# Layer 1's expert weights through one ring of 21 slots, and the gathers between the layers in another order

## What is computed

```python
def moe_ffn(h, router_w, router_b, w_gate, w_up, w_down):
    probs = jax.nn.softmax((h @ router_w).astype(jnp.float32), axis=-1)
    ...                      # the best group of 4 experts, and its top 2
    for e in range(N_EXPERTS):                                   # 16
        y_e = (jax.nn.silu(h @ w_gate[e]) * (h @ w_up[e])) @ w_down[e]
        out = out + combine[:, e:e + 1] * y_e
    return out
```

## Time and profile before

| | |
|---|---|
| median of three runs | 1805.14 us (1793.12 to 1809.05) |
| the profiled execution | 1814.62 us, its span 1813.0 us |
| busy: PE, DVE, ACT, POOL | 92%, 43%, 25%, 17% of the span |
| HBM read, written | 360.55 MB, 29.36 MB |
| layer 0's last block to layer 1's first product | about 1023 to 1066.71 us |
| layer 1's experts | about 1575 to 1799 us |

### The profile page before, as it was taken

One profiled execution on the slowest core, in us unless ns is written; L12 is line 12 of the kernel. 1 busy time (PEld: TensorE's weight loads), 2 busy tenths in 40 slices (PEclk: granted clock), 3 DMA queues, 4 the chain that ended last, 5 costly groups with the idle time before them and its releaser, 6 DMA issues.

```text
span 1813.0 us, 39477 instructions
## 1 busy us (share of the span) xinstructions
PE 1673.1 (92%) x15980; PEld 1064.6 (59%) x15980; DVE 788.7 (43%) x1901; ACT 461.9 (25%) x1015; POOL 303.9 (17%) x298
## 2 busy tenths in 40 slices
PE   5999998989999999999999888999889999899975
PEld 2467555554444444577777556667647888555543
DVE  3578863660110111543444377597664111423222
ACT  4011211552000000444444340111044000333321
POOL 0004341880000000210101210035355000000000
PEclk9999997999999999999999988998689999999998
DMA  9410369509211251489999843125571436599995
GB/s 390 123 67 23 134 243 315 99 18 339 107 69 70 101 224 70 194 328 383 390 383 391 328 172 99 47 84 202 204 140 48 156 146 255 236 392 395 410 410 223
DMA packets 105256, 381.19 MB, mean 210 GB/s; under 512 B 40592, under 2 KB 60304, under 8 KB 66000
## 3 DMA queue, kind: packets, MB, share of 16 engines
q1 hardware_dynamic: 85360, 335.44, 49.6%
q0 software_dynamic: 5648, 33.16, 5.3%
q10 hardware_dynamic: 14128, 10.85, 2.3%
HBM read 360.55 MB, written 29.36 MB: 215 GB/s over the span
## 4 chain that ended last, share of the span: by engine, by line
PE 75%; DVE 6%; DMA 6%; POOL 4%; SPq 3%; issue 3%; ACT 2%; ACTq 0%; DVEq 0%; POOLq 0%
PE tile_ps L661 61%; PE out_ps L661 6%; PE turn_ps L661 5%; SPq L573 3%; POOL arena L2189 3%; DMA h<-in_wpack 2%; DMA vn<-in_wpack 1%; PE turn_ps L986 1%; DMA ring<-in_wpack 1%; DVE arena L2008 1%; DMA x<-in_xT 1%; DVE smx L1990 1%; DVE arena L2100 1%; ACT arena L1459 1%; PE tile_ps L880 0%
## 5 line engine op out<-in xcount | busy, mean ns | idle before, releaser
L661 PE MATMUL tile_ps<-h,ring 128*128 128x512 f32 (+1 forms) x1312 | 478.0, 520 | 5.3 <-ACT h L1236 5.3
L661 PEld LDWEIGHTS tile_ps<-h,ring 128*128 128x128 f32 x1312 | 254.5, 195 | 212.4 <-issue 196.4
L661 PE MATMUL tile_ps<-arena,ring 128*128 128x512 f32 (+1 forms) x704 | 235.3, 486 | 2.4 <-issue 2.4
L661 PE MATMUL tile_ps<-arena 128*32 128x256 f32 (+2 forms) x3136 | 198.7, 341 | 9.1 <-DMA arena<-u_scratch 4.0
L661 PEld LDWEIGHTS tile_ps<-arena,ring 128*128 128x128 f32 x704 | 133.6, 190 | 95.3 <-issue 86.3
L661 PEld LDWEIGHTS tile_ps<-arena 128*32 128x32 f32 (+1 forms) x3136 | 132.0, 119 | 41.9 <-issue 10.3
L2189 POOL TENSOR_SCALAR arena<-arena,smx 128x512 f32<-128x512 f32 (+1 forms) x96 | 128.9, 1361 | 76.4 <-DVE smx L1996 76.1
L1431 ACT ACTIVATE arena<-tile_ps 128x512 f32<-128x512 f32 (+1 forms) x56 | 27.4, 490 | 347.3 <-PE tile_ps L661 347.3
L2030 DVE TENSOR_TENSOR arena<-tile_ps,arena 128x512 f32<-128x512 f32 (+1 forms) x32 | 17.9, 558 | 212.1 <-PE tile_ps L661 212.1
L661 PE MATMUL out_ps<-arena 64*128 64x64 f32 (+2 forms) x1032 | 95.6, 346 | 11.1 <-issue 10.9
L661 PEld LDWEIGHTS out_ps<-arena 64*128 64x128 f32 (+2 forms) x1032 | 77.9, 219 | 19.1 <-issue 19.0
(11 more groups left out here) (360 smaller groups left out, 2479.6 us busy)
## 6 DMA issues: line engine op xcount, KB each, us to landing
ring<-in_wpack SPq DMA_DIRECT2D x176, 1024.0 KB, 8.4
arena<-in_wpack SPq DMA_DIRECT2D x64, 1024.0 KB, 16.6
h<-in_wpack SPq DMA_DIRECT2D x15, 1024.0 KB, 20.1
qa<-in_wpack SPq DMA_DIRECT2D x12, 1024.0 KB, 16.9
qn<-in_wpack SPq DMA_DIRECT2D x12, 1024.0 KB, 18.9
kn<-in_wpack SPq DMA_DIRECT2D x12, 1024.0 KB, 20.8
vn<-in_wpack SPq DMA_DIRECT2D x12, 1024.0 KB, 23.6
x<-in_wpack SPq DMA_DIRECT2D x5, 1024.0 KB, 15.4
```

Of the source, the lines that this page charges most:

```text
L661: return nc.tensor.matmul(out, lhsT, rhs, start=start, stop=stop)
```

## The change

1. `FIFO`: layer 1's expert loads go through one ring of 21 slots in the order of use: load i lies in slot i mod 21. To the 18 slots come three: a dead piece of `arena` with the keys and values of grouped attention; the first 1024 columns of the constants with the working rows; the buffers of roots and squares with a quarter of `h`. Each is filled by two transfers of 512 KB. For this, small tiles are joined (`kv`, `work`, `roots`) and the constants are reordered so that those that are dead by then come first. Warm-up products read other columns of the constants.
2. Load i waits for the gate and up products, or the down products, of the expert that held slot i mod 21 before. Loads 18 and 19 wait for nothing but the router's tables, load 20 for `spread_full`.
3. Layer 1's ring slots 0 and 1 are loaded behind the late gathers too (`n == 0` where `n == 2` stood).
4. POOL issues three soon gathers, waits for `last_out`, then two late, the fourth soon, two late.
5. `load_root`: a root of one constant into a spare column, on ACT, behind the experts' loop of either layer.

```diff
+EXTRA = 3
+FIFO = SHELVES * RING + EXTRA
...
+        def fifo(i):
+
+            slots = (ring_slots + twin + rest_of[1] + extra_slots)[i % FIFO]
+            on, n, turn = i % FIFO // RING, i % FIFO % RING, i // FIFO
+            if on == SHELVES:
+                return slots, extra_in[n], 32 * (turn + 1)
...
-                    if l and n == 2:
+                    if l and n == 0:
                         for t in range(NTOK // P):
                             sp.wait_ge(rows_in[t], 16)
...
+                if l:
+                    freed = None
+                    for e in range(SHELVES, NEXP):
+                        weights = weights_of(sp, e)
+                        for n in range(RING):
+                            i = e * RING + n
+                            if i == FIFO - 1:
+                                sp.wait_ge(spread_full, 2)
+                            if i >= FIFO:
+                                held, part = divmod(i - FIFO, RING)
+                                if (held, part // 4) != freed:
+                                    freed = held, part // 4
+                                    sp.wait_ge((gu_full, down_full)[part // 4][l], before(sp, held + 1))
+                            slot, arrived, _ = fifo(i)
+                            if i % FIFO < SHELVES * RING:
+                                load(slot, arrived, weights + (first + n_static + n))
+                                continue
+                            for half in range(2):
+                                src = wpack[bass.ds(weights + (first + n_static + n), 1), :, half * D:(half + 1) * D]
+                                sp.dma_start(slot[half], src.rearrange("a p (k n) -> (a p) k n", k=4)).then_inc(arrived, 16)
+                    break
...
+            def load_root():
+
+                A(spare[:], c("eps"), ACT.Sqrt)
...
+                load_root()
                 for k in range(KD):
                     act.wait_ge(moe_done, l * NTOK // P * KD + k + 1)
...
+                load_root()
                 act.wait_ge(by_turn_done, 1)
...
+                for t in tiles[:3]:
+                    gather_soon(t)
+                pool.wait_ge(last_out, 16)
+                for t in tiles[:2]:
+                    gather_late(t)
+                gather_soon(tiles[3])
+                for t in tiles[2:]:
+                    gather_late(t)
```

More of the change, by code:

```diff
@@ L320, in backbone @@
         amuls = sb("amuls", [P, LAYERS, 2, KD, 2])
[L321 to L324 removed]
+        work = sb("work", [P, D])
+        csil, qrt, mrow = work[:, 0:256].rearrange("p (k n) -> p k n", k=KD), work[:, 256:512], work[:, 512:]
+        roots = sb("roots", [P, 2 * NTOK])
+        rstd, qsq = roots[:, 0:NTOK], roots[:, NTOK:]
         qrs = rstd
         raw = rstd
[L327 removed]
         qg8 = sb("qg8", [P, 1])
@@ L414, in backbone @@
         ht, a7 = cut(third + SLOT - NTOK // P * D, [NTOK // P, D])
-        assert early_slots <= a7 - NTOK // P * D and a8 <= a7 - NTOK // P * D and a7 - LAT // P * D <= third
+        spare_rows = a7 - NTOK // P * D - D
+        assert early_slots <= a7 - NTOK // P * D and a8 <= spare_rows and a7 - LAT // P * D <= third
         flat = lambda v: v[:].rearrange("p k n -> p (k n)")
@@ L435, in backbone @@
         diag = qsq[:].rearrange("p (t n) -> p t n", n=P)
+        in_quarters = lambda v: v.rearrange("p (k n) -> p k n", k=4)
+        extra_slots = [[in_quarters(arena[:, spare_rows:spare_rows + D]), in_quarters(kv[:])],
+                       [in_quarters(con[:, 0:D]), in_quarters(work[:])],
+                       [in_quarters(roots[:]), h[:, KD // 2:, CTX:]]]
         place_rows, part_rows, place_diag, part_diag = (h[:, k:k + 2, CTX:] for k in range(0, KD, 2))
@@ L556, in backbone @@
         ring_slots = [ring[:, n, :] for n in range(RING)]
+        def fifo(i):
[3 more added lines that the diff above has]
+                return slots, extra_in[n], 32 * (turn + 1)
+            if on == 0:
+                return slots, slot_in[n], 16 * (loads_before(1, n) + static_loads(1, n) + turn + 1)
+            in_layer_0 = sum(shelf(k)[0] == on for k in range(NEXP))
+            return slots, (twin_in, rest_in)[on - 1][n], 16 * (in_layer_0 + turn + 1)
         const_dram = const
@@ L757, in arrived @@
                 def arrived(e, n):
-                    pe.wait_ge(*shelf_in(l, e, n))
-                    slot = shelf_slots(l, e)[n]
-                    return slot if len(slot.shape) == 3 else slot.rearrange("p (k n) -> p k n", k=KD if n < 4 else 2)
+                    slot, here, loads = fifo(e * RING + n)
+                    pe.wait_ge(here, loads)
+                    if isinstance(slot, list):
+                        return lambda k: slot[k // 4][:, k % 4]
+                    v = slot if len(slot.shape) == 3 else slot.rearrange("p (k n) -> p k n", k=KD)
+                    return lambda k: v[:, k]
                 def pick_rows(r):
@@ L806, in down @@
                             for n in range(4):
-                                ins = mm(y[group(n)], hidT1[:, f, group(half)], slots[half][:, f, n * 256:(n + 1) * 256],
+                                ins = mm(y[group(n)], hidT1[:, f, group(half)], slots[half](4 * f + n),
                                          half + f == 0, half + f == 2)
@@ L2258, in _, with gather_soon @@
                 signal(4)
-                for t in tiles:
+                def gather_soon(t):
                     pool.indirect_dma_start(soon_rows[t], None, sorted_out,
@@ L2262, in _, with gather_late @@
                         .then_inc(soon_in[t], 16)
-                pool.wait_ge(last_out, 16)
-                for t in tiles:
+                def gather_late(t):
                     pool.indirect_dma_start(late_rows[t], None, sorted_out,
```

23 lines of the change are left out of this document (10 added, 13 removed).

## The result

The changed kernel took 1780.09 us in the median of 20 runs (1771.62 to 1807.99), the kernel before 1798.39 (1788.56 to 1810.58), 20 runs beside it. The ratio is **0.9885, 95% interval 0.9863 to 0.9908**: 1.15% faster, some 20.7 us of 1798 (the two medians lie 18.3 us apart). The forecast was 1790.0, within 1%; the time lies inside its range, and just on the other side of the 1% line.

The account below looks back on a forecast made before the run. In layer 1's experts PE ends up fed by the DMA stream alone, which bounds it. Ring 7.5 + seam 5.1 + table loads 2.6 = 15.2 us, 0.84% off the 1805.14 median, gives 1790.0 us; range 1777 to 1801.

Parts of the forecast that it names:

- The ring: Layer 1's experts: three extra slots let the weight stream start earlier, gaining 7.5 us.
- Two stalls stayed: PE's 5.88 us stall before expert 13 goes; those before experts 14 and 15 stay about as long.
- The halves: Extra slots' 24 loads of 512 KB in the experts' stream: charged nothing; rival of 7.9 us lost, chance 0.09.
- The seam: Between the layers: 5.1 us gained besides the table load; rival that layer 1 takes it back, chance 0.08.
- The store: POOL's last store at the seam lands in 2.9 us instead of 6.49; rival that it is no sooner, chance 0.18.
- The dummy root: At the seam, ACT's table load moves into its wait for the first gather, removing 1.28 us.
- DVE's second wait: At the seam, DVE's 0.83 us wait for PE's transposes shrinks by 0.3 us.
- The place in the order: At the seam, the first late gather issued one place sooner gains 1.27 us of the 4.8.
- ACT's store: Last block's store at the seam, awaited before the first late gather: 2.5 to 3.3 us beside gathers.
- The end: Behind the last block, the dummy root takes ACT's table load off the chain, gaining 1.28 us.
- PE's clock: Fuller clock at the seam's transposes counted within 0.3 us at DVE's second wait; no gain counted elsewhere.
- the far side: Whole kernel faster by over 1%, 18 us: chance 0.31, half of the forecast's own 0.62.

Follow-up runs that it names:

- c3: Kernel before with the new layout and three extra slots for layer 1's expert weights only, seam and table loads as before; ratio to before 0.9981.
- c5: The changed kernel, no edit, measured again beside the kernel before on another chip; ratio 0.9908.
- d1: The changed kernel, no edit, measured a third time beside the kernel before; ratio 0.9924.
- e1: The changed kernel, no edit, measured a fourth time beside the kernel before; ratio 0.9910.
- e2: The changed kernel plus four warm-up products at PE's 4.6 us gap in layer 1's mixer; ratio to the kernel before 0.9913.
- c1: Control: the kernel before, unchanged, against itself; ratio 1.0005.
- c2: Kernel before with only the joined tiles, reordered constants and warm-up products reading other columns, all loads as before; ratio to before 0.9992.
- c6: Kernel before with one edit, layer 1's first two loads held until behind the gathers; ratio to before 1.0008.
- c12: The changed kernel with the gathers in the old order, four soon ones first; ratio to the kernel before 0.9891.
- c8: Kernel before with only the two dummy roots (early table loads) added; ratio to before 0.9945.
- after: The changed kernel as first measured and profiled; 1780.09 us, ratio to the kernel before 0.9885.
- c10: The changed kernel without its three extra slots, so 18 instead of 21; ratio to the kernel before 0.9923.
- c4: Kernel before with the seam's part only: held layer 1 loads, new gather order and both dummy roots; ratio to before 0.9945.
- d3: The changed kernel without the dummy root at the seam, with 8 warm-up products instead of 5 before layer 1's first product; ratio to before 0.9908.
- d4: The changed kernel with nine more warm-up products at PE's waits in layer 1's mixer; ratio to the kernel before 0.9890.
- c7: Kernel before with only the new gather order (three soon, two late, one soon, two late); ratio to before 0.9982.
- d2: The changed kernel without the dummy root at the seam, the one at the end kept; ratio to the kernel before 0.9923.
- c9: Kernel before with only seven more warm-up products on PE, ahead of its waits for the gathers and layer 1's root; ratio to before 0.9978.

## Why the prediction came out as it did

**The ring: right, 7.5 forecast, about 7.** Expert 13's stretch is 23.8 us in the mean of eight traces with 18 slots turning, and 16.7 over the ten with 21 (all loads but the extra slots' whole). What returns is the stall of 5.88 us plus 1.1, which goes to PE's lower clock behind it (0.50 in 1752:1756; argued, not isolated). Two stalls stayed, as forecast, and the stream ran on at its old rate. Of the third, which the forecast had gone, 0.8 to 1.7 us were left in five of the ten traces (c3, c5, d1, e1, e2), each time for the first extra slot; where nothing was left the stretch is 16.0 and the gain 7.8. The halves, charged at nothing, cost about 1 us of it.

**The seam: right in its first cause, about 1 us less than forecast.** 5.1 + 1.28 = 6.4 were forecast; the four traces of the changed kernel have 25.6 us where c1, c2 and c3 have 30.9: 5.3. The store landed in 2.3 to 2.7 us (forecast 2.9), but that gave less than the forecast's 3.5: behind its issue the first late gather goes 2.5 us sooner than in c1 to c3 (8.2 and not 10.7 us), since the one trace read had the store at 6.49 and these at 5.1 to 5.3. The late gather itself brought 1.1 us that nobody had counted: DVE's first sum stands 5.3 us behind its issue and not 6.4. So 3.7 us in place of 4.8. By itself the hold is worth 4.0 with PE's clock (c6). The dummy root gives its 1.28, and DVE's second wait its 0.3 (3.13 us in the mean of the four, 3.41 before). The place in the order, counted at 1.27, gives nothing beside the other two (c12), because POOL then waits for ACT's store. The prediction's own times say as much: its three gathers are out at 1031.4 and the late one waits until 1033.0, so the fourth fits between. ACT's store took 3.5 to 4.0 us in the changed kernel, above the 2.5 to 3.3 that the prediction allowed for.

**The end: wrong.** "Both removed: 2.6 us" took the table load for 1.28 us at both places. At the end it gave 0.18 us (c8, and the trace of after). The rows of the chain put ACT's load behind ACT's squares; they did not show that PE's 16 products of these squares would be the next to hold the root. In the kernel before they stand at

```profile
1800.70 3.69 PE L661 MATMUL tile_ps<-h,con 128*128 128x256 f32 x16 [1.15 <-ACT h L1314]
```

and end at 1804.39, some 0.2 us before the load (1803.31 + 1.28). This is the term most plainly mis-sized: the prediction didn't name what is late next there, as it did elsewhere.

**PE's clock: the step that failed the most.** The prediction counted it at DVE's second wait alone, 0.3 us, and put it at nothing everywhere else, without a reason. By waits the three parts make 7 + 5.3 + 0.2 = 12.5 us, and four measurements 17.6 (15 to 20). The 5 us between go with the granted clock. Over all 333 timed runs of this study the time falls by 14.7 us for 0.01 of mean granted clock (one slope fitted over all runs, with a level for each kernel on each chip; scatter 2.5 us around it). At one clock the changed kernel and c12 are 8.6 to 10.8 us faster than the kernel before beside them, and the ring 6.0 (c3 against before, and again c12 against c10). The other 7 to 8 us of the 17.6 are the 0.0049 to 0.0055 by which the clock was granted higher (c5, d1, e1). About 1.4 us of them lie in the terms counted above (0.3 at DVE's second wait, 1.1 behind the stall of expert 13), up to 3 in the first products behind the root (the windows of c1 and c8). This is a correlation and no more: single kernels lie off it, c4 at one clock 2.8 us faster than before where its waits make 5.6, c8 5.1 where they make 1.5.

The table's column points to an edit: the clock rose by 0.0030 to 0.0078 in every kernel in which PE's gap for the root was shortened, by the dummy or by idle products alone (c4, c5, c8 to c12, d1, d3, d4, e1, e2), and by -0.0018 to +0.0009 in those where it was left (c1, c2, c3, c6, c7). d2, with the gap open but the rest of the change, is the exception at +0.0031. The twenty traces agree in part. In the 4 us from PE's first product behind that gap the granted clock was 0.50 to 0.65 in all seven traces with a gap of 3.6 us. With 2.0 us it was 1.00 in seven of eleven, and 0.57 to 0.73 in c4, c10, d4 and e1. With 1.0 us it was 1.00 in both (c9, d3). So the dummy root at the seam was probably worth more than its 1.28 us, and c8's timing says so (both dummies, 4.0 us at least, where the waits give 1.5); how much more is not settled, since d2 against d1 shows no loss, and that the clock is the cause of the whole 5 us is not shown.

**What stays open.** Where between the seam and the experts the clock falls differs from one execution to the next, also of one program ("rest" is 120.8 and 111.5 in two traces of the kernel before). The four traces of the changed kernel are shorter there by 3.4 us in the mixer and 1.4 in "rest" than c1, c2 and c3 in the mean; whether that follows from the seam or is what this scatter makes of so few was not told apart. The timed ratios can't tell: their intervals are 4 to 7 us to either side.

**The chances.** The sum was 3 us short of the 1% line, and 0.31 for the far side was half of the forecast's own chance. The four measurements, one beyond the line and three within it, say that this was about the right doubt.

## What to carry to other kernels

Before a wait is priced at its full length, ask what would have released the same instruction next: a table load beside the last reduction and a gather behind somebody else's store gave 0.2 and 0 us of the 1.28 and 1.27 they showed on the chain. A small store on the critical path wants no megabytes of loads in flight beside it, even on another queue. Slots that let a saturated stream start sooner return nearly their whole transfer time (7 of 7.5 us). And where the rows show PE at its 1.2 GHz level behind a gap, a shorter gap may be worth more than the wait, but only timed runs tell, not one trace.

## What the runs showed of the hardware beyond that

- One program's clock differs by execution: the kernel before took 1784.2 to 1823.51 us over 130 runs on five chips beside the experiments, and within one chip most of that goes with the granted clock.
- The same gap of PE was not always followed by the same clock: behind the 2.0 us for the root PE ran at 1.00 in seven traces and at 0.57 to 0.73 in four, one of them the changed kernel itself (e1).
- POOL's store of one block took 5.0 to 6.5 us with two 1 MB loads of SP's queue under way, which had been issued 23 us earlier, and 2.3 to 2.7 us without them. DVE's first sum stood 5.1 to 5.5 us behind the issue of the first late gather in after, c5, d1 and e1, and 6.3 to 6.5 in the four traces of the old seam.
- Halves of 512 KB in a stream bound by bytes ran at 392 GB/s against 404 for whole loads.
